# Convolution input, layer norm output and MLP input transposed by DMA instead of TensorE and VectorE, in a hybrid decoder block

## What is computed

```python
u = rms_norm(h, mix_pre_g)
proj = u @ w_in                          # 2*1024 glu, 1024 pool, 2*1024 gates
y_conv = swish(layer_norm(dwconv31(a * sigmoid(gate)) + bias)) @ w_conv_out
y_pool = (trailing means - p, per-group linear, scale) @ w_pool_out
merged = g_conv * y_conv + g_pool * y_pool
h = h + rms_norm(merged @ w_o, mix_post_g)
v = rms_norm(h, mlp_pre_g)
v = jnp.square(jax.nn.relu(v @ w_ff1)) @ w_ff2
h = h + rms_norm(v, mlp_post_g)
```

## Time and profile before

| | |
|---|---|
| median of 3 runs | 981.34 us (979.9 to 1103.43) |
| the profiled execution | 980.87 us |
| its span, slowest core (7) | 979.3 us |
| spans of the 8 cores | 976.0 to 979.3 us |
| TensorE busy | 960.4 us, 98% of the span |
| VectorE, ScalarE, POOL busy | 413.8, 338.3, 34.8 us |
| matmuls and transposes on TensorE | 5246 records |

### The profile page before, as it was taken

How to read it: one execution, slowest core, us unless ns; L and a number is a source line. 1 busy time by engine, 2 the same in 40 slices (tenths; PEclk the granted TensorE clock), 3 DMA queues, 4 the chain that set the end, 5 groups by cost and what they waited for, 6 DMA issues and landing times.

```text
span 979.3 us, 15429 instructions; the slowest of 8 cores (976.0 to 979.3 us)
## 1 busy us (share of the span) xinstructions
PE 960.4 (98%) x5246; PEld 491.7 (50%) x5246; DVE 413.8 (42%) x671; ACT 338.3 (35%) x606; POOL 34.8 (4%) x50
## 2 busy tenths in 40 slices
PE   5999999999999999999999999999999999999997
PEld 3555666776554544444444444444444444444443
DVE  3464233334558213565555542254323542245222
ACT  3565223112112861464554331034211431034211
POOL 3000000000000000010101000000000000000000
PEclk9999999999999999999999999999999999999999
DMA  9999403656669008739597991340131301330021
GB/s 193 215 218 180 69 1 53 108 93 101 109 110 198 2 8 143 130 103 222 139 204 166 201 192 44 87 131 20 34 103 59 109 22 44 83 111 23 1 83 68
DMA packets 62175, 102.33 MB, mean 104 GB/s; under 512 B 10353, under 2 KB 42353, under 8 KB 62098
## 3 DMA queue, kind: packets, MB, share of 16 engines
q0 software_dynamic: 32608, 46.45, 31.8%
q1 hardware_dynamic: 24880, 53.31, 17.4%
q10 hardware_dynamic: 4610, 1.58, 0.6%
HBM read 127.78 MB, written 16.84 MB: 148 GB/s over the span
## 4 chain that ended last, share of the span: by engine, by line
PE 97%; DMA 1%; DVE 1%; ACT 0%; issue 0%; DVEq 0%; SPq 0%; ACTq 0%
PE ps L329 95%; PE ps L332 2%; DMA arena<-xh 1%; DVE arena L362 0%; ACT junkb L342 0%; DVE xb L352 0%; ACT arena L342 0%; DVE arena L352 0%; DVEq L173 0%; DVE tmpA L345 0%; SPq L365 0%; DVE sm L356 0%; ACT sm L342 0%; DVEq L140 0%; ACTq L140 0%
## 5 line engine op out<-in xcount | busy, mean ns | idle before, releaser
L329 PE MATMUL ps<-arena 128*128 128x512 bf16 (+2 forms) x4528 | 915.9, 364 | 4.1 <-DVE arena L362 2.9
L329 PEld LDWEIGHTS ps<-arena 128*128 128x128 bf16 x4528 | 450.2, 104 | 456.8 <-issue 6.1
L342 ACT ACTIVATE tmpA<-ps 128x512 f32<-128x512 f32 x226 | 133.3, 595 | 298.8 <-PE ps L329 264.6
L345 DVE TENSOR_TENSOR arena<-tmpA 128x512 bf16<-128x512 f32 x128 | 86.6, 691 | 77.7 <-ACT tmpA L342 77.6
L345 DVE TENSOR_TENSOR arena<-ps,tmpA 128x512 bf16<-128x512 f32 x64 | 43.9, 690 | 147.0 <-ACT tmpA L342 127.8
L342 ACT ACTIVATE junkb<-ps 128x512 bf16<-128x512 f32 x64 | 38.2, 597 | 163.2 <-DVE tmpA L345 108.5
L342 ACT ACTIVATE junkb<-arena 128x1024 bf16<-128x1024 f32 (+1 forms) x33 | 34.7, 1053 | 98.6 <-DMA arena<-xb 87.9
L342 ACT ACTIVATE arena<-ps 128x512 bf16<-128x512 f32 (+2 forms) x68 | 43.5, 651 | 52.5 <-PE ps L329 32.6
L356 DVE RECIPROCAL sm<-sm 128x1 f32<-128x1 f32 (+1 forms) x65 | 10.3, 159 | 107.6 <-ACT sm L342 107.1
L345 DVE TENSOR_TENSOR tmpA<-ps,gbt 128x512 f32<-128x512 f32 x64 | 44.1, 688 | 20.5 <-PE ps L329 19.6
L352 DVE SCALAR_TENSOR_TENSOR arena<-tmpA,sm,arena 128x1024 f32<-128x1024 f32 (+1 forms) x33 | 41.2, 1252 | 24.8 <-DMA arena<-out 20.5
(11 more groups left out here) (43 smaller groups left out, 196.0 us busy)
## 6 DMA issues: line engine op xcount, KB each, us to landing
arena<-xh SPq DMA_DIRECT2D x32, 512.0 KB, 9.6
arena<-w_ff POOLq DMA_DIRECT2D x16, 1024.0 KB, 25.4
out<-arena SPq DMA_DIRECT2D x31, 512.0 KB, 3.0
arena<-convw POOLq DMA_DIRECT2D x16, 768.0 KB, 6.6
arena<-out SPq DMA_DIRECT2D x16, 512.0 KB, 3.8
arena<-out SPq DMA_DIRECT2D x48, 128.0 KB, 3.8
arena<-w_in POOLq DMA_DIRECT2D x4, 1024.0 KB, 67.7
arena<-w_in POOLq DMA_DIRECT2D x2, 2048.0 KB, 23.2
```

What stands on the lines that cost most here:

```text
L329: kb.op("pe", lambda e: e.matmul(out_ap, lhsT=lhsT, rhs=rhs, start=start, stop=stop, skip_group_check=skip), reads=reads, writes=writes)
L342: kb.op("act", lambda e: e.activation(out=out_ap, in_=in_ap, func=func, **kw), reads=reads, writes=writes)
L345: kb.op(eng, lambda e: e.tensor_tensor(out=out_ap, in0=in0, in1=in1, op=op), reads=reads, writes=writes)
```

## The change

Three kinds of transposes go to transposing DMAs, all issued from SP by a new helper `DTR`:

- `cv_t2`: one transfer of 128 x 2048 bf16 (512 KB) per channel block instead of 16 transposes and two evictions. UT's rows grow from 130 to 144 columns, the halo columns have a key of their own. Two of them are issued ahead of the stage, and the first `cv_mm` comes after the fourth piece of the main work (`interleave` with lead 3).
- `cv_t3`: one transfer per channel block (for blocks 3 and 7 two halves) into four buffers, and the SiLU is an own step, `cv_silu`, which reads SBUF. The side work of the layer norm lies in groups 12 to 19. Transfers 0 to 3 are issued ahead of group 20; the SiLU pairs come after groups 23, 26, 29 and 31; transfers 4 and 5 behind the first pair, 6 and 7 behind the second.
- `h_transp`: one transfer of 128 x 1024 (256 KB) per token tile, in the E stage and in the MLP, where it takes the place of `s6_transp` and `s6_spread`; one load of 128 rows takes that of four. hT is laid out with 512 contiguous tokens per k.

Beside that: in block 0 of `gate_conv` three gate halves are issued ahead of the first y half; the last tile of the MLP is done in parts of 512, 256 and 256 columns, its two stores on SP and ScalarE; UH and the halo staging move into the free first half of `gb`. Of the diff, registrations of ranges and renamed parameters are left out:

```diff
@@ -206,12 +206,15 @@
...
         xs = aview(OFF_C, 6 * 2048).bitcast(F32).rearrange("p (b n) -> p b n", b=6)
-        UTt = [aview(OFF_C + b * 2080, 2080, g=16, m=130) for b in range(2)]
-        Wc = [aview(OFF_C + 4160 + b * 3072, 3072, g=8, d=3, n=128) for b in range(3)]
+        UTt = [aview(OFF_C + b * 2304, 2304, g=16, m=144) for b in range(2)]
+        Wc = [aview(OFF_C + 4608 + b * 3072, 3072, g=8, d=3, n=128) for b in range(3)]
         wgc = aview(OFF_C, 8192, k=8, n=1024)
...
         xt = [aview(o, 2048).bitcast(F32) for o in XT_OFF]
-        hT = aview(OFF_S, 4096, s=16, k=8, t=32)
+        t3v = [[aview(XT_OFF[0], 2048, r=16, m=128)], [aview(XT_OFF[1], 2048, r=16, m=128)],
+               [xb[:, 0:2, :].rearrange("p b (r m) -> p (b r) m", m=128)],
+               [xb[:, 2, :].rearrange("p (r m) -> p r m", m=128), aview(OFF_C + 12288, 1024, r=8, m=128)]]
+        hT = aview(OFF_S, 4096, k=8, t=512)
         pwf = arena[:, OFF_Z:OFF_Z + Z_N].bitcast(F32).rearrange("p (k t) -> p k t", k=8)[:, :, 0:256]
...
@@ -364,6 +377,9 @@
...
 
+        def DTR(out_ap, in_ap, reads, writes):
+            return kb.op("sp", lambda e: e.dma_start(out=out_ap, in_=in_ap, transpose=True), reads=reads, writes=writes, dma=True)
+
         def wload(sl_ap, src_ap, keys, after=()):
...
@@ -631,17 +642,9 @@
...
             bf, h = cc % 2, cc // 4
-            for half in range(2):
-                b = nb()
-                psb = ps[:, b, :].bitcast(BF16)
-                for g8 in range(8):
-                    gl = half * 8 + g8
-                    TR(psb[:, g8 * 128:(g8 + 1) * 128], ru[:, cc, gl * 128:(gl + 1) * 128], identb[:],
-                       ([("utm", h, r) for r in range(16)] if cc % 4 == 0 else []) + [("um", cc), "identb"], [PSK(b)])
-                COPY("act" if half else "dve", UTt[bf][:, half * 8:half * 8 + 8, 2:130], psb.rearrange("p (g m) -> p g m", g=8),
-                     [PSK(b)], [("UT", bf)])
-            COPY("dve", UTt[bf][:, :, 0:2], UH[:, h, :, 16 * (cc % 4):16 * (cc % 4) + 16].rearrange("p m g -> p g m"),
-                 [("UH", h)], [("UT", bf)])
+            DTR(UTt[bf][:, :, 16:144], ru[:, cc, :], [("utm", h, r) for r in range(16)] + [("um", cc)], [("UT", bf)])
+            COPY("dve", UTt[bf][:, :, 14:16], UH[:, h, :, 16 * (cc % 4):16 * (cc % 4) + 16].rearrange("p m g -> p g m"),
+                 [("UH", h)], [("UTh", bf)])
 
...
@@ -650,8 +653,8 @@
...
                 for d in range(3):
-                    MM(ps[:, b, g4 * 128:(g4 + 1) * 128], UTt[bf][:, gl, d:d + 128], Wc[w % 3][:, gl % 8, d, :], d == 0, d == 2,
-                       [("UT", bf), ("Wc", w % 3)], [PSK(b)])
+                    MM(ps[:, b, g4 * 128:(g4 + 1) * 128], UTt[bf][:, gl, 14 + d:142 + d], Wc[w % 3][:, gl % 8, d, :], d == 0, d == 2,
+                       [("UT", bf), ("UTh", bf), ("Wc", w % 3)], [PSK(b)])
             dst = ru[:, cc, :].rearrange("p (r g c) -> p g r c", r=16, g=16)[:, q * 4:q * 4 + 4, :, :]
...
@@ -677,14 +680,18 @@
...
         def cv_t3(cc):
-            bb = (nb(), nb())
-            for r in range(16):
-                psb = ps[:, bb[r // 8], :].bitcast(BF16)
-                TR(psb[:, (r % 8) * 128:(r % 8 + 1) * 128], ru[:, cc, r * 128:(r + 1) * 128], identb[:], [("nr", r), "identb"], [PSK(bb[r // 8])])
+            i = cc % 4
+            for h in range(2 if i == 3 else 1):
+                n = 8 if i == 3 else 16
+                DTR(t3v[i][h], ru[:, cc, h * n * 128:(h + 1) * n * 128], [("nr", r) for r in range(16)], [("t3", i, h)])
+
+        def cv_silu(cc):
+            i = cc % 4
             sv = ru[:, cc, :].rearrange("p (m r) -> p m r", r=16)
-            for half in range(2):
-                ACT(sv[:, :, 8 * half:8 * half + 8], ps[:, bb[half], :].bitcast(BF16).rearrange("p (r m) -> p m r", r=8), AF.Silu,
-                    [PSK(bb[0]), PSK(bb[1]), "vec"], [("s", cc)], bias=vcol(8, cc), scale=vcol(0, cc))
+            for h, t in enumerate(t3v[i]):
+                n = 16 // len(t3v[i])
+                ACT(sv[:, :, h * n:(h + 1) * n], t.rearrange("p r m -> p m r"), AF.Silu,
+                    [("t3", i, k) for k in range(len(t3v[i]))] + ["vec"], [("s", cc)], bias=vcol(8, cc), scale=vcol(0, cc))
 
...
@@ -700,19 +707,35 @@
...
 
-        def gate_conv(blk, cc):
-            bg, by = nb(), nb()
+        def gate_conv_g(blk, cc):
+            bg = nb()
             for kc in range(8):
...
                    ["uT", "wgc"], [PSK(bg)])
+            t_i = nti(4 if blk == 0 else 2)
+            ACT(tmpA[:, t_i, :], ps[:, bg, :], AF.Sigmoid, [PSK(bg)], [("tmpA", t_i)])
+            return t_i
+
+        def gate_conv_y(blk, cc, t_i):
+            by = nb()
             for kc in range(8):
...
                    [("s", kc), "wco"], [PSK(by)])
-            t_i = nti(2)
-            ACT(tmpA[:, t_i, :], ps[:, bg, :], AF.Sigmoid, [PSK(bg)], [("tmpA", t_i)])
             m1 = zt[:, cc, blk * 512:(blk + 1) * 512]
...
             TTOP("dve", m1, tmpA[:, t_i, :], m1, ALU.add, [("tmpA", t_i), ("m1", blk, cc)], [("m1", blk, cc)])
+
+        gate_ahead = []
+
+        def gate_conv(blk, cc):
+            if blk == 0:
+                if cc == 0:
+                    gate_ahead.extend(gate_conv_g(0, c) for c in range(3))
+                elif cc < 6:
+                    gate_ahead.append(gate_conv_g(0, cc + 2))
+                gate_conv_y(0, cc, gate_ahead.pop(0))
+            else:
+                gate_conv_y(blk, cc, gate_conv_g(blk, cc))
 
...
@@ -754,15 +777,20 @@
...
         main.insert(1, lambda: glu_halo(1))
-        interleave(main, conv_pieces(range(4)))
+        side0 = conv_pieces(range(4))
+        side0.pop(0)()
+        side0.pop(0)()
+        interleave(main, side0, 3)
         halo_t(1)
...
         for n, r in enumerate(range(16)):
-            side1.insert(2 * n + 2, lambda r=r: ln_stat(0, r))
-        interleave(groups[:12], side1)
+            side1.insert(2 * n + 3, lambda r=r: ln_stat(0, r))
+        side1.pop(0)()
+        side1.pop(0)()
+        interleave(groups[:12], side1, 3)
         wload(S[1][:, :, :], wco_v, ["wco"], after=[kb.last_write[("Wc", 0)]])
...
@@ -777,20 +805,27 @@
...
                 [lambda q=q: ln_b(range(4 * q, 4 * q + 4)) for q in range(4)]
-        interleave(groups[12:21], side2)
+        interleave(groups[12:20], side2)
 
...
 
+        def silu_pair(i):
+            cv_silu(2 * i)
+            cv_silu(2 * i + 1)
+
         DMA("sp", gb[:, 1, :], gbd[1:2, :].partition_broadcast(128), [], [("gb", 1)])
         DMA("sp", gb[:, 0, :], gbd[2:3, :].partition_broadcast(128), [], [("gb", 0)])
-        for i in range(4):
-            groups[21 + 2 * i]()
-            t3_pair(i)
-            groups[22 + 2 * i]()
-        for f in groups[29:]:
-            f()
+        t3_pair(0)
+        t3_pair(1)
+        for n in range(20, 32):
+            groups[n]()
+            if n in (23, 26, 29, 31):
+                i = (n - 22) // 3
+                silu_pair(i)
+                if i < 2:
+                    t3_pair(i + 2)
         wload(S[2][:, :, :], wo_v, ["wo"])
...
@@ -837,8 +865,8 @@
...
         def h_transp(j, bi):
-            transp_part(128, bi, lambda b, psb: COPY(
-                alt(), hT[:, 4 * j:4 * j + 4, :, :], psb.rearrange("p (k s t) -> p s k t", k=8, s=4), [PSK(b)], [("hTp", j)]))
+            tl = j % 4
+            DTR(hT[:, :, tl * 128:(tl + 1) * 128], xb[:, bi, :], [("xb", bi)], [("hT", tl)])
 
...
@@ -875,39 +903,49 @@
...
 
-        def s6_load(blk, x):
-            for q in range(4):
-                DMA("sp", xt[0][32 * q:32 * q + 32, :], omain[4 * blk + q][32 * x:32 * x + 32, :], [("outh", 4 * blk + q)], [("xq", q)])
+        def s6_load(j):
+            DMA("sp", xt[0], omain[j], [("outh", j)], [("xt", 0)])
 
         def s6_norm():
-            return norm_part(128, xt[0], [("xq", q) for q in range(4)], 0)
-
-        def s6_transp(x, bi):
-            bo = next_xb()
-            kb.op("dve", lambda e: e.transpose(xb[:, bo, :].rearrange("p (c k t) -> p k c t", c=4, k=8),
-                                               xb[:, bi, :].rearrange("p (k c t) -> p k c t", k=8, c=4)),
-                  reads=[("xb", bi)], writes=[("xb", bo)])
-            return bo
-
-        def s6_spread(x, bo):
-            for q in range(4):
-                for c in range(4):
-                    DMA(("sp", "act")[c % 2], hT[32 * c:32 * c + 32, 4 * q + x, :, :].rearrange("p k t -> p (k t)"), xb[32 * q:32 * q + 32, bo, 256 * c:256 * c + 256],
-                        [("xb", bo)], [("hT", x, q, c)])
-
-        def ff1_unit(fc, hkeys):
+            return norm_part(128, xt[0], ("xt", 0), 0)
+
+        def ff1_unit(fc):
             b = nb()
...
             for kc in range(8):
-                MM(ps[:, b, :], wv[:, kc, fl * 128:(fl + 1) * 128], hT[:, :, kc, :], kc == 0, kc == 7,
-                   [("ff1", c)] + (hkeys if kc in (0, 7) else []), [PSK(b)])
```

(45 more changed lines are left out.)

## The result

| | before | changed |
|---|---|---|
| median | 981.23 us | 1047.72 us |
| ratio, 95% interval | | 1.0656 (1.0632 to 1.068) |
| profiled execution | 980.87 us | 1044.99 us |
| span, slowest core | 979.3 us (core 7) | 1043.4 us (core 3) |

Each median includes one slow execution (1103.43 and 1209.01 us); the ratio is of the others alone, 979.9 to 981.34 us before and 1041.57 to 1050.45 changed.

The account below looks back on a forecast made before the run. TensorE was taken to bound the kernel; -16.1 (transposes) - 0.35 (end) + 1.0 (convolution) + 1.9 (layer norm) = -13.5 us from 980.87 us, median forecast 967.5 us, range 960 to 1015 us.

Parts of the forecast that it names:

- What bounds the kernel, and what leaves TensorE: TensorE, busy 98%, sets the time; 288 transposes at 0.056 us leave its queue, -16.1 us.
- The end: After the last matmul: shorter square and earlier reciprocal, against 64 narrower matmuls, net -0.35 us.
- What one transfer costs: 512 KB transposing DMA: t, time from one transfer to the next, 3.5 us; landing 1.5 more; slow bound 17 us.
- Convolution input: Convolution stage: transfers mostly hidden, sharing DMA engines with weight loads; +1 us of TensorE stall.
- the time until a buffer is needed: Convolution stage: shortest time from a buffer being free to its need is 13 us; alone a transfer may take 8.
- Layer norm output: After the layer norm: last SiLU pair ends at 49.9 us, TensorE is ready at 48.1; stall +1.9 us.
- MLP: MLP and E stage: half-length transfers stay hidden, as their use lies far behind; 0 us.
- R1: Rival: transfer ring becomes the bound, t of 5 to 10 us; 972 to 1021 us, chance 0.28.
- R2: Rival: transfer paced by its pieces, t = 17; 98 us after layer norm, 37 in convolution; about 1100 us, chance 0.18.
- R4's remark on the clock: Rival that the change doesn't take TensorE's time, excluded; lower clock after stalls would cost more, but half-idle first slice kept full clock.

Follow-up runs that it names:

- run 9: Changed kernel with convolution input and layer norm output both transposed on TensorE again, keeping the MLP input by DMA, gate halves ahead and new ending: 978.64 us, 0.9976.
- run 5: Changed kernel with a narrower read list, convolution transfers and POOL's weight loads waiting for each other, and the w_in load behind transfers 0 and 1: 997.83 us, 1.017.
- Runs 3: Changed kernel without the 13 convolution weight loads from w = 3 on (stale weight tiles used): 995.5 us, 1.0144.
- runs 7 and 8: Changed kernel with convolution weights from w = 3 on made bf16 beforehand, loaded without a cast from ScalarE's queue (989.57 us), then from POOL's (1003.92 us).
- run 1: Changed kernel with convolution transfers listing the gated products as read only for a half's first channel block: 1037.62 us, 1.0567.
- run 7: Changed kernel with convolution weights from w = 3 on made bf16 beforehand and loaded without a cast from ScalarE's queue: 989.57 us, 1.008.
- run 2: Changed kernel with the convolution input transposed by TensorE again, in the order of the kernel before: 986.42 us, 1.0043.

## Why the prediction was wrong, point by point

- **What bounds the kernel, and what leaves TensorE** (-16.1 us): right. 288 transposes are gone, and where little else happens (the MLP in run 9) the time falls by about what they cost. Their evictions were 20, not 18; that changes nothing.
- **The end** (-0.35 us): too high. The square takes 0.38 us and the product 0.42 instead of 0.60 and 0.69, but the reciprocal did not come ahead of the product: the product stands before it in VectorE's queue and starts at 1038.87 us, the reciprocal at 1039.21. From the end of the last matmul to the reciprocal it is 1.64 us before, 1.65 in the changed kernel and 1.43 in run 9. So the end gives nothing here and 0.2 us there, less the 0.1 us of the narrower matmuls.
- **What one transfer costs** (t = 3.5 us, 1.5 us more to land): right where the transfer is alone. After the layer norm one follows the other every 2.2 to 3.2 us and lands in 4.3 to 6.3 us. The figure of the Trainium skill (DMA: Bandwidth & Descriptors, Latency and other measured facts), 261 GB/s, from which I estimate 2.0 us for 512 KB, is near the lower end of this. The 1309 ns per block of the Trainium skill (VectorE: DVE Perf Modes, The three transpose paths) don't multiply: by them I estimate 21 us, and sixteen blocks take 2.2 to 3.2 us here. But the bounds failed: I put 17 us as the slow end, from small transfers in a quiet stage, and transfer 6 took 45.1.
- **Convolution input** (+1 us): this is the step that failed, by 60 us of waiting and 7 us of slower clock. It said that "the transfer should not fill all 16 engines" and that with serial sharing the stall at t = 4 is 5.8 us. A serial model is near where transfers and loads do go one after the other: run 5 leaves 14.6 us of stalls, inside the 12 to 16 that such a model gave for it. What it could not hold is that side by side with POOL's loads both get slower: 16.3 us for transfer 0, 34.6, 23.3, 45.1 and 35.8 for 2, 3, 6 and 7, a median of 21 for the loads, and 76 GB/s written at a DMA share of 1.32. Runs 3 and 5 show that the loads beside them are the cause, runs 7 and 8 that POOL's queue is a large part of it. I had the DMA share of 0.58 to 0.62 before my eyes and read it as room. Such a share does not say what two kinds of transfer do to each other. The cover that I counted for transfer 0 (9.9 us) also left out that the 2 MB w_in load runs beside it.
- **In the same step**, the time until a buffer is needed (13 us) was read from TensorE's order alone. The diff gives the reads of the whole half to every transfer, where the kernel before gave them to the first block only, and thereby a wait to VectorE in front of the bias additions. That is some 9 us of the 60 (run 1).
- **Layer norm output** (+1.9 us): the mechanism was right, the last SiLU pair is what TensorE waits for, releaser and place as forecast (6.65 and 3.61 us; the 0.89 us ahead of them, behind VectorE, were not); the size was off. The term is the SiLU from SBUF: "I leave it at that" was 2.45 us, it measures 3.9. The waits came to 11.2 us, and 3.3 us of slower clock follow them, for which the sum had no term.
- **MLP** (0 us): right (run 9), and it held although two transfers took 16 us beside w_ff loads.
- **The rivals.** The slow side was right in sign with R1 and R2, but both placed the loss in a ring after the layer norm, which ran at t of 2.2 to 3.2 us. Contention in the convolution was named only as an extra of 0 to 24 us. The time came out between R1's end, 1021, and R2's 1100. R4's remark on the clock was too light: the first slice, half idle at full clock, did not tell what 6 to 33 us of waiting would do.

With the measured terms the sum is -16.1 + 61.4 + 11.2 + 7.0 + 3.3 - 2.6 (start) = +64.2, and 64.1 were measured. It closes because 7.0 and 3.3 are the remainders of the two stretches; what speaks for them is TensorE's busy time above.

## What to carry to other kernels

Before work moves to the DMA engines, list what else is in flight at that very place, and from which queue: a transfer that takes 4 us alone may take ten times that beside another queue's loads, and a busy share of 0.6 does not exclude it. A saving of 0.056 us per transpose on TensorE is small against what can go wrong; it pays, if at all, where the result is needed long after the transfer (MLP input) or nothing else moves beside it (the first two convolution blocks). Where the loads can't be moved, another queue for them helps: with bf16 weights from ScalarE's queue some 57 of the 64 us of loss went (run 7), though such weights have to be made ahead of the kernel. And when an operand changes its home or its stride, the reader's price is to be taken from a row with that home and stride.

## What the runs showed of the hardware

- A transposing DMA of 512 KB from SBUF to SBUF lands in 4.3 to 5.1 us with no load beside it (up to 6.3 close behind another one), in 6.8 (median) beside plain loads of ScalarE's queue, in 15.0 beside the same loads of POOL's queue, in 10.3 beside one casting load of POOL's, and in 23.3 to 45.1 where two transfers meet three of those. These loads of 768 KB go from 6.5 us to 21 to 39 there. One of 256 KB takes 3.1 us at best and 16 beside POOL's w_ff loads.
- ScalarE, 2048 bf16 columns: 2.1 us read in order and written in runs of 32; 3.9 read with a stride of 256 bytes from SBUF and written in order (the same stride from PSUM, written in runs of 8: 2.4; from SBUF, written in such runs: 4.2); 9.0 read in order and written with a stride of 32 bytes.
- TensorE with a moving operand of 2-byte elements at a stride of 64 bytes: 372 matmuls, about 150 of them of this kind, take 200 us instead of about 80, at a granted clock of 0.69.
- In and after a wait of 6.7 us the granted clock was 0.50 (run 2, 371 to 376 us), and the mean over the convolution stage with its waits was 0.83.
